# Five reorderings in a hybrid decoder layer: key copies, low parts, last gates, query products and a transpose

## The reference, cut to what matters

```
h = rmsnorm(x); q_a, c, kr, z_attn, z_ssm, xbc, dt = split(h @ w_in)
q = rmsnorm(q_a) @ w_q_b;  ckv = rmsnorm(c);  k_rope = rope(kr)
scores[h] = (q_nope[h] w_uk[h]^T . ckv + rope(q)[h] . k_rope) * scale, causal
o[h] = softmax(scores[h]) @ ckv @ w_uv[h] * silu(z_attn)
y = ssd(conv(xbc), dt) + d_skip * xs;  y_ssm = group_rmsnorm(y * silu(z_ssm))
out = x + rmsnorm(concat(o, y_ssm) @ w_out)
```

## Time and profile before

| | value |
|---|---|
| median of three runs | 500.34 us |
| the profiled execution: its own time | 500.38 us |
| its span, first to last instruction | 498.6 us |
| TensorE matmuls busy | 483.7 us (97%) |
| TensorE weight loads busy | 423.7 us (85%) |
| VectorE busy | 351.4 us (70%) |
| ScalarE busy | 283.0 us (57%) |
| GpSimd busy | 92.6 us (19%) |
| mean granted TensorE clock | 0.997 |

### The profile page before, as it was taken

The page is one execution under the profiler, slowest core; times in us unless marked ns, Lnnn a source line. Parts: engine busy times, 40 slices in busy tenths (PEclk is TensorE's granted clock), DMA queues, the critical chain, the costliest instruction groups (busy, mean ns, idle before and its releaser), DMA issues.

```text
span 498.6 us, 12380 instructions
## 1 busy us (share of the span) xinstructions
PE 483.7 (97%) x4756; PEld 423.7 (85%) x4756; DVE 351.4 (70%) x795; ACT 283.0 (57%) x580; POOL 92.6 (19%) x122
## 2 busy tenths in 40 slices
PE   8999999999999999999999998999899999999995
PEld 7999999999999999999999874666566689998883
DVE  4653768693857567555433599698999799998763
ACT  6733412234376474654624995677776869764441
POOL 1641000010000010000000142544555701110500
PEclk9999999999999999999999999999999999999998
DMA  8543222469898989979896331733322676799842
GB/s 284 216 170 122 72 74 96 133 196 359 296 321 285 310 286 306 325 263 326 296 309 219 121 93 53 252 124 115 133 89 95 239 254 208 245 316 388 329 130 84
DMA packets 47852, 106.34 MB, mean 213 GB/s; under 512 B 7881, under 2 KB 13794, under 8 KB 47666
## 3 DMA queue, kind: packets, MB, share of 16 engines
q1 hardware_dynamic: 47650, 105.50, 62.6%
q10 hardware_dynamic: 144, 0.05, 0.1%
HBM read 96.27 MB, written 7.75 MB: 209 GB/s over the span
## 4 chain that ended last, share of the span: by engine, by line
PE 73%; DVE 15%; ACT 5%; issue 3%; POOL 2%; SPq 1%; DMA 1%; DVEq 0%; ACTq 0%; POOLq 0%
PE pm L1794 17%; PE pm L1795 16%; PE pm L1796 16%; PE px L1905 3%; PE px L1930 3%; DVE hring L1430 3%; PE px L2092 2%; DVE u L1180 2%; PE px L1795 1%; PE px L1796 1%; PE px L1794 1%; PE pm L2110 1%; DVE w_lo L1087 1%; POOL hring L1741 1%; PE pm L2080 1%
## 5 line engine op out<-in xcount | busy, mean ns | idle before, releaser
L1794 PE MATMUL pm<-xw_hi,w_lo 128*128 128x260 f32 x520 | 150.5, 289 | 0.0
L1795 PE MATMUL pm<-xw_lo,w_hi 128*128 128x260 f32 x520 | 147.0, 283 | 0.0
L1796 PE MATMUL pm<-xw_hi,w_hi 128*128 128x260 f32 x520 | 146.9, 282 | 0.0
L651 ACT ACTIVATE w_hi<-w_raw 128x1024 fp32r<-128x1024 f32 (+1 forms) x70 | 72.5, 1038 | 81.2 <-PE pm L1796 65.4
L1087 DVE TENSOR_TENSOR w_lo<-w_raw,w_hi 128x1024 fp32r<-128x1024 f32 (+1 forms) x70 | 87.8, 1261 | 31.6 <-ACT w_hi L651 31.5
L1794 PEld LDWEIGHTS pm<-xw_hi,w_lo 128*128 128x128 f32 x520 | 98.0, 188 | 1.6
L1795 PEld LDWEIGHTS pm<-xw_lo,w_hi 128*128 128x128 f32 x520 | 97.9, 188 | 0.1
L1796 PEld LDWEIGHTS pm<-xw_hi,w_hi 128*128 128x128 f32 x520 | 97.9, 188 | 0.0
L1794 PE MATMUL pm<-mix_hi,w_lo 128*128 128x264 f32 x128 | 37.2, 291 | 0.8 <-DVE mixlo_a L1485 0.8
L783 ACT ACTIVATE alpha<-nmh 128x1 f32<-128x1 f32 x16 | 4.7, 295 | 56.1 <-DVE nmh L1193 56.1
L1796 PE MATMUL pm<-mix_hi,w_hi 128*128 128x264 f32 x128 | 36.3, 284 | 0.0
(11 more groups left out here) (315 smaller groups left out, 1098.9 us busy)
## 6 DMA issues: line engine op xcount, KB each, us to landing
page<-in_cache SPq DMA_DIRECT2D x128, 288.0 KB, 4.2
w_raw<-in_w_in SPq DMA_DIRECT2D x32, 512.0 KB, 5.1
w_raw<-in_w_out SPq DMA_DIRECT2D x16, 512.0 KB, 3.9
w_raw<-in_w_tok SPq DMA_DIRECT2D x16, 512.0 KB, 5.8
dec<-ac_dram SPq DMA_DIRECT2D x16, 256.0 KB, 3.6
hring<-in_ssm_state SPq DMA_DIRECT2D x8, 512.0 KB, 6.6
o_ssms<-hring SPq DMA_DIRECT2D x8, 512.0 KB, 6.9
w_raw<-in_w_qb SPq DMA_DIRECT2D x6, 384.0 KB, 2.9
```

The source lines that it names most:

```text
L651: act.activation(w_hi[s][:, 0:n], w_raw[s][:, 0:n], ACT.Copy).then_inc(a_whi, 1)
L1794: pe.matmul(out, wl, xh, start=start, stop=False)
L1795: pe.matmul(out, wh, xl, start=False, stop=False)
L1796: return pe.matmul(out, wh, xh, start=False, stop=stop)
```

## The change: five edits of order

Nothing is added or removed; five things stand at other places in their engine's list.

1. Stage 1, TensorE: `query_lat` is issued two steps of k (six matmuls) later within item 18.
2. Stage 2, VectorE: `stack_low(2)` and `stack_low(3)` leave steps 6 and 7 and come after `state(7)`, `head(3)` and `head(4)`; TensorE's `bct` transpose moves ahead of `keys(0)` and the last chunk state.
3. Stage 3, VectorE: `stack_low(7)` moves from the end of `y_pair(0)` to behind `head(5)` in the loop's first turn.
4. Stage 3, ScalarE: `copy_k(s + 2)` goes ahead of `exps(s + 1, 3)`, the fourth exponentials, in each turn of the loop that has one (s = 0 to 5).
5. Start of stage 4, ScalarE: `gated_square(7)` goes behind the last two `copy_pt`, and `mix_high(7)` ahead of `ssm_high(0)`; VectorE: `mix_low(7)` goes ahead of `group_scale(2)`.

```
 scalar:
-            exps(s + 1, 3)
             if s + 2 < H:
                 copy_k(s + 2)
+            exps(s + 1, 3)
...
-        gated_square(7)
         mix_high(H - 2)
         copy_pt(H - 1, 2)
         copy_pt(H - 1, 3)
+        gated_square(7)
+        mix_high(H - 1)
         ssm_high(0)
-        mix_high(H - 1)
 vector:
-            if n in (6, 7):
-                stack_low(n - 4)
         state(2 * NCH - 1)
         for h in range(3, 5):
             head(h)
-        stack_low(4)
-        stack_low(5)
+        for h in range(2, 6):
+            stack_low(h)
...
         y_pair(0)
-        stack_low(7)
...
                 head(5)
+                stack_low(7)
...
         gated(H - 1)
+        mix_low(H - 1)
         group_scale(2)
-        mix_low(H - 1)
 tensor:
-                    if (i, r, k) == (18, 0, 3):
+                    if (i, r, k) == (18, 0, 5):
                         query_lat()
...
+        pe.wait_ge(a_cvs, 2)
+        pe.wait_ge(v_cb, 2)
+        pe.transpose(px[0:32, 3, 0:P], cvs[:, 1, 8:12, :], cm[:, M_ID, :]).then_inc(p_bct, 1)
         pe.wait_ge(v_xdt, 2 * NCH)
         keys(0)
         state(2 * NCH - 1)
-        pe.wait_ge(a_cvs, 2)
-        pe.wait_ge(v_cb, 2)
-        pe.transpose(px[0:32, 3, 0:P], cvs[:, 1, 8:12, :], cm[:, M_ID, :]).then_inc(p_bct, 1)
         pe.wait_ge(a_bct, 1)
```

## The result

The changed kernel takes 507.11 us (median of four runs, 506.35 to 507.6) against 500.32 for the kernel before (500.05 to 502.52): a ratio of 1.0124, 95% interval 1.0093 to 1.0156. The profiled execution took 507.6 us (span 505.8). The sign was right, and so were the two steps on which the forecast rests, a longer hold of ScalarE and a fall of TensorE's clock; the time lies above the range, whose upper end was 504.8. In two later groups of runs the same kernel measured 505.65 and 505.69 beside 501.27 and 501.29, ratios 1.0093 [1.0077, 1.0108] and 1.0094 [1.0077, 1.0110], which are 4.7 us of 500.34 or 505.0: just above that end, which the intervals (504.2 to 505.8) take in.

What follows compares the result with a forecast made beforehand. VectorE was taken to bound the end of stage 2 and the heads' loop, TensorE stages 1 and 4. Profiled 500.38 + 1.75 (work) + 1.6 (clock) = 503.7 us, chance 0.38; range 499.2 to 504.8.

Steps and rivals of the forecast that it cites:

- the clock term: End of stage 2: TensorE's 4.5 us stop likelier than not lowers its clock; +1.6 us, between nothing and 2.3.
- part 1: Stage 1, query products: TensorE's 0.72 us wait for VectorE's last rotary product goes, nothing else moves; -0.7 us.
- Part 2: End of stage 2: ScalarE held longer for `stack_low(3)`, delaying the transpose's copy and TensorE's output rows by 2.95 us.
- Part 3: Stage 3: moving low part 7 cuts the shift to +2.2, repaid by `head(7)`; with Part 2, taken +2.8 us.
- Part 4: Heads' loop, key copy: turn 0's delay covered, turns 2 to 4 gain nothing, turn 5 gains; -0.55 us.
- Part 5: Start of stage 4, last gates: VectorE about 0.5 sooner at the gate, 0.7 later by idle time; +0.2 us.
- The sum of the work: All five edits without the clock: -0.7 + 2.8 - 0.55 + 0.2 = +1.75 us.
- The one with the clock holding: Rival: same TensorE wait at the end of stage 2, but no clock fall; 502.1 us, chance 0.29.
- The TensorE-bound loop: Rival: TensorE's wait for keys bounds the heads' loop, the key copy gives back up to 5.1; 497.6 us, chance 0.15.
- The ScalarE wait costs little: Rival: the low-part moves of stages 2 and 3 cost only near +0.3; 499.6 us, chance 0.18.

Runs made afterwards that it cites:

- the kernel with ten matmuls: Changed kernel plus ten matmuls whose results nobody reads, in TensorE's stop before its wait for the copied transpose: 503.17 us, and 502.77 us once more.
- the low part and gates alone: Kernel before with only `stack_low(7)` moved behind `head(5)` and the last gates' order changed: 501.87 us, ratio 1.0009.
- the low parts alone: Kernel before with only `stack_low(2)` and `stack_low(3)` moved behind heads 3 and 4: 506.45 us, ratio 1.0104.
- the key copy alone: Kernel before with only `copy_k(s + 2)` moved ahead of the fourth exponentials: 501.25 us, ratio 1.0000.

## Why the prediction was wrong, and where it was right

**What failed: the size of the clock term, and part 1.** The prediction put the fall at +1.6, "on the side of the only row". By the profiled execution it is (1.94 - 1.11) + (3.52 - 1.98) = 2.37; by the runs, with everything else in place, 2.5 and 2.9. Its own bound was 2.3, from the slow pace over the first 4.63 us. That row was the length of ten matmuls (five in the code, each shown as two passes), not that of the slow stretch: here the low level lay over some 5 us of work, from 312.1 to about 317.1. The row to use was the full 2.3, with more above it. (The granted clock reads 1.00 over those first matmuls, so that they ran slow is read from the pace alone: 0.46 us a pass of 256 columns against 4.53 / 20 = 0.23 in the kernel with ten matmuls.)

The traces give the price once more. From the first chunk state of stage 2 to the first maximum of head 0 it takes 30.30 us in both kernels with ten matmuls, 32.67, 32.80 and 33.23 in three traces with the changed kernel's order there and a low level of 6.8 to 6.9 us, and 31.69 and 31.75 in two where it lasted 3.4: 2.4 to 2.9, and 1.4.

The forecast took the fall as likelier than not, and it came: 1.00 to 0.50 within a stop of 4.56 us, where the stop of 1.85 us had left 1.00. The Trainium skill, "TensorE: Matmul & The Clock Gate", section "HAM oscillation — how this bites in real kernels", says that waits between bursts of matmuls throttle the clock and that the next burst starts cold; these rows agree. But 1.85 us is no safe length: behind the same stop the clock fell in the trace of the low part and gates alone (0.57 over 353 to 357).

**Part 1** was -0.7 and came to nothing: TensorE came to the query products later but arrived sooner at the cache page behind them, whose load wasn't there (0.2 to 1.1 us in traces with the edit that show the wait). "Nothing else moves" left out what TensorE meets next; a page wait of 0.3 turns up in one trace without the edit too. Nor is it the page alone: TensorE reaches the first chunk state of stage 2 anywhere from 283.86 to 285.61 us over the traces with the edit and from 284.49 to 285.34 over those without, and at 285.28 in the changed kernel without the edit, which shows no page wait. What else moves it stays open.

**Part 2** held: a ScalarE wait near 6.6 was forecast, 6.52 came; the copy moved by 3.94, of which 0.99 is a later arrival from stage 1 (VectorE's add at 307.64 against 306.65 in the working), so 2.95 is the hold, as forecast. The earlier transpose gained nothing while ScalarE was held: from the first chunk state to the output rows it is 26.48 us with it and, in the kernel with the low parts alone, without it.

**Part 3** held in kind: `head(7)` decides in turn 1, as the rows of the first two turns show. In size it missed: the shift is 6.30 at the first maximum and 6.60 at `head(7)`, 0.3 more, where the forecast had it shrink by 0.15.

**Part 4** was -0.55 and is 0.00 [-0.6, +0.6] alone, where turn 0 lacks the moved low part as cover. Waits for probabilities in place of those for keys, and turns 11 us long, are as forecast. Behind the last state update the gain is there: -0.49 in the trace of the key copy alone.

**Part 5** was +0.2; the trace of the low part and gates alone shows +0.20 in the same stretch. With both parts and the weight in time it is 34.08 to 34.13 against 34.37, or -0.24 to -0.29, where -0.35 was forecast. The first trace of the changed kernel lost this again, as the first output weight landed late there.

**The sum of the work**, +1.75, is near what the two kernels with the clock held measure: 503.17 - 501.27 = 1.9 and 502.77 - 501.29 = 1.5. With 2.5 to 2.9 for the clock that makes the 4.4 of both repeats. Some runs of the kernel before have a fall of their own (last section); against the others, with medians of 501.07 and 500.32, the work is 2.1 and 2.4.

**Left open:** the first four runs lost 6.8, not 4.4. Their one trace can be laid beside the forecast, 7.2 against 3.35 us. Of the 3.9 between them, 1.8 lie in stage 1 (it reaches stage 2 1.1 later than the kernel before, where 0.7 sooner was forecast), 0.8 in the clock, 0.3 between the first maximum and `head(7)`, and 1.0 behind it, where the late weight is. The repeats reach stage 2 at 284.00 and 284.54, not 285.61, and lose less to the weight (waits of 0.69 and 0.34, not 1.37). Whether the other three first runs were like the traced one isn't on record, and the intervals of the ratios (1.0093 to 1.0156, 1.0077 to 1.0110) overlap.

**Rivals.** The one with the clock holding (502.1) needed that no fall comes, and every trace of the changed kernel has one; with the clock held by hand the kernel came to 503.17 and 502.77. The TensorE-bound loop was ruled out by the key copy alone. "The ScalarE wait costs little" was ruled out by the low parts alone.

## What to carry to other kernels

When an edit delays one engine's step, look for the instruction of another engine that stands in order behind it, and list what is queued there: here a copy of 0.27 us, wanted by TensorE, stood behind a high part that wasn't wanted for another seven heads. Move that one, and the edit is harmless here. And where a new stop of TensorE is longer than any in the trace that left the clock at its upper level, price the work behind it at half pace for as long as a fall lasted in a trace (3.4 to 6.9 us here), not for a share of that. Look at the mean granted clock of every run too: one profile without a fall doesn't show that the kernel has none.

## What was not expected of the hardware

The same stop of 4.56 us cost differently from one execution to the next. The clock fell in the stretch of 310 to 312 both times, but in one it stayed low for 1.8 + 4 + 1.1 = 6.9 us (the rows at 0.56, 0.50 and 0.86), in the other for 1.8 + 1.6 = 3.4 us (0.55 and 0.80), and the loss on rows and keys was 2.37 and 0.83 + 0.61 = 1.44 us. Sixteen matmuls that nobody reads kept the clock at 1.00 as well as useful ones do.

The kernel before has falls too, though its profile shows none. In the 18 traces a mean granted clock of 0.995 or less comes only with a fall ahead of the last matmul. Of the 91 runs of the kernel before in the four groups, 42 are at 0.995 or less, with a median of 501.6 us against 500.9 for the rest. With the key copy moved, which takes away the stop of 1.85 us, none of 12 runs is. So the key copy's new place goes with a clock that stays up in the loop, which the prediction did not count; where the clock fell in those 42 runs isn't traced.
